# Splitting each unit's wait: products with the high weight part first, those with the low part in the last third

## The reference

```
xn = rmsnorm(h, norm_mix_g)
p_rw, q, c_kv, iq, ik, iw, gates = split(xn @ w_in)         # 2048 -> 9480
h = h + (g_a * (y_a @ w_branch_rwkv) + g_b * (y_b @ w_branch_dsa)) @ w_out
act = gelu(hx . expert_u[e]);  h = h + sum_k gate * act * expert_v[e]   # both expert tables are multiplied whole
q, fz, i, gate = split(rmsnorm(x) @ a_w_in);  x = x + o @ a_w_out
k, v, f = split(rmsnorm(x) @ kv_w);  q, gate = split(rmsnorm(x) @ b_w_in);  x = x + o @ b_w_out
```

## Time and profile before

| what | value |
|---|---|
| median of 3 runs | 3644.63 us |
| profiled execution | 3647.17 us, of which the span from first to last instruction is 3645.0 us |
| granted TensorE clock, mean of the span | 0.983 of full speed |
| PE, matmuls | busy 3546.6 us, 97% of the span, 20474 instructions |
| PE, weight loads | busy 3012.9 us, 83% (they lie beside the matmuls) |
| DVE / ACT / POOL | 59% / 48% / 9% |

### The profile page before, as it was taken

One profiled execution on the slowest core, in us unless ns is written; L12 is line 12 of the kernel. 1 busy time (PEld: TensorE's weight loads), 2 busy tenths in 40 slices (PEclk: granted clock), 3 DMA queues, 4 the chain that ended last, 5 costly groups with the idle time before them and its releaser, 6 DMA issues. The chain is left out here.

```text
span 3645.0 us, 50852 instructions
## 1 busy us (share of the span) xinstructions
PE 3546.6 (97%) x20474; PEld 3012.9 (83%) x20474; DVE 2155.3 (59%) x2871; ACT 1752.3 (48%) x2613; POOL 342.6 (9%) x217
## 2 busy tenths in 40 slices
PE   8998999889999999999999999999999999999999
PEld 6777777678799999888899998887788887788777
DVE  4776555646566487655544465555678885555454
ACT  5453333424444577444444444444555554444763
POOL 0000000000069700000000000000022210000000
PEclk9999999999999999999999999999999999999999
DMA  6554333445545455555555565555544335455334
GB/s 224 176 191 143 116 125 131 160 168 195 189 171 184 173 174 175 193 210 187 193 208 184 207 255 207 207 188 178 175 141 142 133 131 186 177 190 191 127 139 162
DMA packets 111180, 638.55 MB, mean 175 GB/s; under 512 B 17738, under 2 KB 23658, under 8 KB 39192
## 3 DMA queue, kind: packets, MB, share of 16 engines
q1 hardware_dynamic: 106664, 622.98, 48.1%
q0 software_dynamic: 4336, 13.14, 1.1%
HBM read 611.10 MB, written 21.54 MB: 174 GB/s over the span
## 5 line engine op out<-in xcount | busy, mean ns | idle before, releaser
L222 DVE TENSOR_TENSOR lo_w<-ring,hi_w 128x1024 fp32r<-128x1024 f32 x500 | 612.4, 1225 | 989.1 <-ACT hi_w L216 981.2
L216 ACT CAST hi_w<-ring 128x1024 fp32r<-128x1024 f32 x540 | 569.0, 1054 | 958.2 <-DMA ring<-in_wstream 933.6
L224 DVE TENSOR_TENSOR lo_w<-ring,hi_w 128x1024 fp32r<-128x1024 f32 x500 | 612.0, 1224 | 0.0
L1998 PE MATMUL PS<-hi_x,hi_w 128*128 128x256 f32 x2048 | 580.4, 283 | 3.2 <-POOL lo_w L224 3.2
L1998 PE MATMUL PS<-hi_x,lo_w 128*128 128x256 f32 x2048 | 573.9, 280 | 0.0
L1998 PE MATMUL PS<-lo_x,hi_w 128*128 128x256 f32 x2048 | 569.5, 278 | 0.0
L217 ACT CAST hi_w<-ring 128x1024 fp32r<-128x1024 f32 x540 | 564.8, 1046 | 0.0
L2024 PE MATMUL PS<-hi_w,hi_g 128*128 128x512 f32 x1024 | 404.0, 395 | 1.0 <-issue 1.0
L2024 PE MATMUL PS<-lo_w,hi_g 128*128 128x512 f32 x1024 | 403.5, 394 | 0.0
L2024 PE MATMUL PS<-hi_w,lo_g 128*128 128x512 f32 x1024 | 403.2, 394 | 0.0
L1998 PEld LDWEIGHTS PS<-hi_x,hi_w 128*128 128x128 f32 x2048 | 384.8, 188 | 3.6 <-ACT GG L2238 3.5
(11 more groups left out here) (583 smaller groups left out, 5780.0 us busy)
## 6 DMA issues: line engine op xcount, KB each, us to landing
ring<-in_wstream SPq DMA_DIRECT2D x540, 1024.0 KB, 4.8
other_G<-staged SPq DMA_DIRECT2D x32, 256.0 KB, 6.1
hot<-other_G SPq DMA_DIRECT2D x8, 1024.0 KB, 6.9
gates_dram<-gst POOLq DMA_DIRECT2D x8, 512.0 KB, 4.8
x_dram<-x SPq DMA_DIRECT2D x2, 2048.0 KB, 12.0
x<-x_dram SPq DMA_DIRECT2D x2, 2048.0 KB, 9.5
prev<-RKV POOLq DMA_DIRECT2D x6, 508.0 KB, 5.4
x<-in_x SPq DMA_DIRECT2D x4, 512.0 KB, 6.5
```

The costliest lines, as they stand in the source:

```text
L216: a.copy(hi_w[s][:, 0:HALF], ring[s][:, 0:HALF]).then_inc(S(f"hi{s}"), 1)
L222: v.tensor_tensor(lo_w[s][:, 0:HALF], ring[s][:, 0:HALF], hi_w[s][:, 0:HALF].bitcast(F32), ALU.subtract)
L224: v.tensor_tensor(lo_w[s][:, HALF:UNIT], ring[s][:, HALF:UNIT], hi_w[s][:, HALF:UNIT].bitcast(F32), ALU.subtract)\
L1998: m = nc.tensor.matmul(PS[:, s, 0:T], wa[s][:, k * P:(k + 1) * P], xa[:, k, :], start=(k == 0 and p == 0), stop=(k == KC - 1 and p == 2))
```

## The change

Two orders of a dense unit's 24 products are added. `p` is now 0: high x high, 1: low activation x high weight, 2: high activation x low weight.

- `order_lo_last`: tile 0 with p = 0, 1 (8 matmuls), tile 1 with p = 0, 1 (8), then p = 2 of tile 0 (4) and of tile 1 (4).
- `order_by_tile`: as `order_lo_last` within each tile: tile 0's 8 and 4, then tile 1's 8 and 4. It is used for the 8 units of the RWKV branch and for the last unit of the final stage (L3108).

Each unit starts with a wait on `hi{slot}` (both halves), and waits on `lo{slot}` right ahead of its first product with p = 2. In expert-u units the 32 products with `hi_w` come first and then the 16 with `lo_w`; in expert-v units the 16 with `hi_w` and then the 8 with `lo_w`, but for the last unit of a v stage, which waits for both at its start and keeps its bank order. The waits on `psum_free` stand, as before, ahead of the first product of a tile; that of tile 1 is now the 9th product of the unit and was the 13th. The number of matmuls and of weight loads is the same; ACT's, DVE's, POOL's and SP's programs are not touched.

```diff
+    order_by_tile = [(tt, k, p) for tt in range(NT) for ps in ((0, 1), (2,)) for k in range(4) for p in ps]
+    order_lo_last = [(tt, k, p) for ps in ((0, 1), (2,)) for tt in range(NT) for k in range(4) for p in ps]
...
             def quarter(u, g):
...
-                    t.wait_ge(S(f"lo{slot}"), u // SLOTS + 1)
+                    t.wait_ge(S(f"hi{slot}"), u // SLOTS * 2 + 2)
...
-                if WIN + 8 <= u < OUT:
-                    t.wait_ge(S("ya_lo"), 2 * q + tt + 1)
...
-                if g % 2 == 0 and q == 0 and 2 * m + tt >= 3:
-                    before = 2 * m + tt - 3
-                    t.wait_ge(S(f"psum_free{before % 2}"), before // 2 + 1)
-                for k in range(2 * (g % 2), 2 * (g % 2) + 2):
+                by_tile = WIN + 8 <= u < OUT
+                for i, (tt, k, p) in list(enumerate(order_by_tile if by_tile else order_lo_last))[6 * g:6 * g + 6]:
+                    if p == 0 and k == 0:
+                        if by_tile:
+                            t.wait_ge(S("ya_lo"), 2 * q + tt + 1)
+                        if q == 0 and 2 * m + tt >= 3:
+                            before = 2 * m + tt - 3
+                            t.wait_ge(S(f"psum_free{before % 2}"), before // 2 + 1)
+                    if p == 2 and k == 0 and tt == 0:
+                        t.wait_ge(S(f"lo{slot}"), u // SLOTS + 1)
...
             def u_unit(g, s, hf, between=()):
                 t.wait_ge(S("gelu_free"), g * 4 + (hf * HK + s + 1))
-                t.wait_ge(S(f"lo{s}"), g + (GROUP[f"u{hf}"] + 1))
-                for k in range(KC):
+                t.wait_ge(S(f"hi{s}"), g * 2 + (GROUP[f"u{hf}"] * 2 + 2))
+                steps = [(k, p) for k in range(KC) for p in range(2)] + [(k, 2) for k in range(KC)]
+                for i, (k, p) in enumerate(steps):
                     for j in between:
-                        if AT[j] % KC == k:
+                        if 3 * (AT[j] % KC) == i:
                             burst(j)
...
+                    if (k, p) == (0, 2):
+                        t.wait_ge(S(f"lo{s}"), g + (GROUP[f"u{hf}"] + 1))
...
             def v_unit(g, s, hf, first=False, last=False, order=(0, 1)):
-                t.wait_ge(S(f"lo{s}"), g + (GROUP[f"v{hf}"] + 1))
+                if last:
+                    t.wait_ge(S(f"lo{s}"), g + (GROUP[f"v{hf}"] + 1))
+                t.wait_ge(S(f"hi{s}"), g * 2 + (GROUP[f"v{hf}"] * 2 + 2))
...
-                    for p, (ga, wa) in enumerate(((hi_g, hi_w), (hi_g, lo_w), (lo_g, hi_w))):
+                    for p, (ga, wa) in enumerate(((hi_g, hi_w), (lo_g, hi_w), (hi_g, lo_w))[0:3 if last else 2]):
...
+                if not last:
+                    t.wait_ge(S(f"lo{s}"), g + (GROUP[f"v{hf}"] + 1))
+                    for tt, c in pairs:
+                        m = nc.tensor.matmul(PS[:, 4 * tt + c, :], hi_g[:, s, tt * P:(tt + 1) * P],
+                                             lo_w[s][:, c * 512:(c + 1) * 512], start=False, stop=False)
...
             def unit(u):
...
-                t.wait_ge(S(f"lo{q}"), (U0 + u) // SLOTS + 1)
+                t.wait_ge(S(f"hi{q}"), (U0 + u) // SLOTS * 2 + 2)
...
+                for tt, k, p in order_lo_last:
+                    if (k, p) == (0, 0):
+                        if u == KU:
+                            t.wait_ge(S("psum_free1"), N0 + KU // SLOTS - 1)
+                        elif q == 0 and 2 * m + tt >= 3:
+                            before = 2 * m + tt - 3
+                            t.wait_ge(S(f"psum_free{before % 2}"), N0 + before // 2 + 1)
+                    if (tt, k, p) == (0, 0, 2):
+                        t.wait_ge(S(f"lo{q}"), (U0 + u) // SLOTS + 1)
```

More of the change, by code:

```diff
@@ L602, in quarter @@
             def quarter(u, g):
-                slot, tt = u % SLOTS, g // 2
+                slot = u % SLOTS
                 if u < WIN:
@@ L1778, in unit @@
                         t.wait_ge(S(f"psum_free{tt}"), N0 + m - 1)
-                t.wait_ge(S(f"lo{q}"), (O0 + w) // SLOTS + 1)
+                t.wait_ge(S(f"hi{q}"), (O0 + w) // SLOTS * 2 + 2)
                 if w >= QU:
                     t.wait_ge(S("xq_lo"), 2 * q + 2)
[L1782 to L1787, removed]
+                for tt, k, p in order_lo_last:
+                    if (tt, k, p) == (0, 0, 2):
+                        t.wait_ge(S(f"lo{q}"), (O0 + w) // SLOTS + 1)
+                    kk = q * 4 + k
+                    xa, wa = ((X_w[0], hi_w), (X_w[1], hi_w), (X_w[0], lo_w))[p]
+                    mm = nc.tensor.matmul(PS[:, 2 * (m % 2) + tt, :], xa[:, kk, tile(tt)], wa[q][:, k * 512:(k + 1) * 512],
+                                          start=(kk == 0 and p == 0), stop=(kk == KC - 1 and p == 2))
                 mm.then_inc(S("unit_used"), 1)
@@ L2132, in a_unit @@
             def a_unit(u):
-                t.wait_ge(S(f"lo{u}"), A0 // SLOTS + 1)
+                t.wait_ge(S(f"hi{u}"), A0 // SLOTS * 2 + 2)
                 t.wait_ge(S("xa_lo"), 2 * u + 2)
-                for tt in range(NT):
-                    for k in range(4):
-                        kk = u * 4 + k
-                        for p, (xa, wa) in enumerate(((hi_x, hi_w), (hi_x, lo_w), (lo_x, hi_w))):
-                            m = nc.tensor.matmul(PS[:, tt, :], xa[:, kk, tile(tt)], wa[u][:, k * 512:(k + 1) * 512],
-                                                 start=(kk == 0 and p == 0), stop=False)
+                for tt, k, p in order_lo_last:
+                    if (tt, k, p) == (0, 0, 2):
+                        t.wait_ge(S(f"lo{u}"), A0 // SLOTS + 1)
+                    kk = u * 4 + k
+                    xa, wa = ((hi_x, hi_w), (lo_x, hi_w), (hi_x, lo_w))[p]
+                    m = nc.tensor.matmul(PS[:, tt, :], xa[:, kk, tile(tt)], wa[u][:, k * 512:(k + 1) * 512],
+                                         start=(kk == 0 and p == 0), stop=False)
                 m.then_inc(S("unit_used"), 1)
```

82 lines of the change are left out of this document (40 added, 42 removed).

## The result

| | before | changed |
|---|---|---|
| median of 6 runs each | 3642.77 us (3640.19 to 3645.78) | 3658.44 us (3651.55 to 3664.55) |
| ratio, 95% interval | | 1.0039 (1.0027 to 1.0050) |
| profiled execution | 3647.17 us, span 3645.0 | 3663.58 us, span 3661.5 |

The change makes the kernel slower: by 14.2 us as the ratio has it, by 15.7 as the two medians have it. The forecast was +0.7 us and its range ended at 3652. The profiled execution of after is 5 us above its median, so its trace shows a little more loss than the usual run has.

What follows compares the result with a forecast made beforehand. PE, busy 97% of the span, was taken to bound the kernel by products times spacing plus idle time. Terms −0.8 + 0 − 3.2 + 4.65 = +0.7 us on the median 3644.63 gave 3645.3 us, range 3636 to 3652.

Steps and rivals of the forecast that it cites:

- The count and spacing of products: All PE matmuls: same number, and the new order leaves their spacing at 0.2316 us, so 0; ±4 us kept for the range.
- The bound of half a nanosecond: Limit on spacing change per product in dense and v units: 15,960 products x 0.5 ns = ±8 us.
- a count in 350 us off by ten or more: Sign of a wrong forecast: L2024 matmuls begun in 350 us leave 1513 by that much, putting product order on the path.
- The wait for tile 1's bank: Chunk starts in L631 and L2606: bank needed at the 9th product, not the 13th; five late waits of 0.93 us, +4.65.
- the clock behind the longer waits: L2606: longer idle time may drop the clock, 1.7 us per stretch, +5.1 us in all; counted in the range alone.
- L637, taken as 0: Tile 1's bank wait in this line (L631 before): late once, at `RKV`, DVE's chain sets PE's next stop; 0, at most +0.9.
- First unit and expert-u stage: PE starts some 1.4 us earlier in the first unit, −0.8; two 1.6 us waits on POOL's `lo_w` go, −3.2.
- Second `lo_w` wait: At 342.87 us: PE is through earlier but stands longer for DVE before L852; 0, other end −5.1 us.
- One more wait per unit: Some 535 added waits on PE: 0 when already met, at most 2.7 us.
- the second rival: Added wait costs even when met, 0 to 0.08 us per unit: 3656 us at 0.02, 3688 at 0.08; chance 0.12.
- The first rival: Gains kept: idle time at 342.87 us does not return at 358.68, first unit brings more; 3638.5 us or less; chance 0.14.
- the third: Rival: PE waits on `lo_w` just the same, at the 17th product, only the bank wait acts; 3649.3 us; chance 0.08.

Runs made afterwards that it cites:

- order_only: Changed kernel with the wait on the low part back at each unit's start, product order and bank waits kept: 3660.2 us, ratio 1.0052 to the kernel before.
- met_wait: Kernel before, order kept, with one more always-met wait on PE in u, v, L2606 and L3108 units: 3646.51 us, ratio 1.0002.
- v_alternate: Kernel before with 124 steady v units reordered so that neither stationary nor moving block stands twice running: 3641.4 us, ratio 0.9993.
- alternate_all: Kernel before with v_alternate's v units, and dense units of five of six lines changing tile, bank and blocks with every product: 3639.78 us, ratio 0.9983.
- pair_order: Kernel before with v_alternate's sequence of high and low weight parts in dense and v units, tiles and banks as before: 3647.78 us, ratio 1.0014.
- v_runs: Kernel before with 124 steady v units ordered tile by tile in runs of four products keeping one stationary block: 3647.92 us, ratio 1.0007.
- dense_only: Kernel before with only the dense units changed as in the changed kernel, expert units as before: 3655.04 us, ratio 1.0029.
- before_swapped: Kernel before, order and waits untouched, with hi_w and lo_w (with its ring) exchanged in on-chip memory: 3642.77 us, ratio 0.9999.

## Why the prediction was wrong

**The count and spacing of products: 0.** This is the step that failed. It was sized from two orders that both alternate high and low weight parts, product by product; I varied tile and bank in my mind, which turned out to be nothing, and not the run of one part. The bound of half a nanosecond was what those two quotients could hide, not what a new order could do, and it was too narrow even for that: one count more or less in the window of 304 is 0.8 ns, and 216 uninterrupted products of the same stage take 50.15 us, 232.2 ns. In its place: +1.26 ns in 3072 v products (300.39/1297 to 300.39/1290), 3.9 us. For dense units two uninterrupted stretches can be compared, 336 products of the key and value stage (77.95 us, now 78.30) and the 216 behind them (50.15, now 50.31): +0.9 ns, for 6744 products 6.2 us if the others do the same. The second u stage adds 0.4 ns in 3072 products, 1.3 us. Together about 11 us, where the forecast kept 4. By runs, exchanging the places takes back 10.6. The forecast's own sign for this, a count in 350 us off by ten or more, was set too far out: 1506 is off by seven.

**The wait for tile 1's bank: +4.65.** Place and price were right: `fz`, `hq` and `x` grew by 0.9, 0.9 and 2.4 us, 4.2 in all. Removed by experiment it is 7.3 us in that stage and 9.8 with L637 (each uncertain by some 5, so 4.65 is not excluded). What I held for the range alone, the clock behind the longer waits, may be the rest: 3.4 us more of missing clock in after's trace, and about 4 by the means of all runs; neither is beyond what kernels without late banks differ by. L637, taken as 0, had 0.9 at `RKV`, and its share of the 1.8 us at L858.

**First unit and expert-u stage: −0.8 and −3.2.** Right: 19.18 us and no wait on POOL; order_only, which gives them up, is 4.7 us slower.

**Second `lo_w` wait: 0.** Right in kind: a chain of DVE sets PE's next start. But the forecast took DVE's chain as independent of when PE is through, and it isn't: PE's earlier end lets SP load the next unit earlier, that load meets the transfer that DVE waits for, and PE starts 1.8 us later than before. So this term was a loss and not 0.

**One more wait per unit: 0.** Right (met_wait, 1.0002), and with it the second rival fell. The rule of the Trainium skill that weight loads are pulled ahead ("TensorE: Matmul & The Clock Gate", Part 2, step by step) would have let one doubt it; by this case's trace no load was laid bare at a met wait, 1296 products against 1297. The first rival fell with the 12.3 us wait, the third with the 0.8.

The sum with measured terms: −4.7 (splits) + 10.6 (spacing, by place) + 9.8 (banks, with clock) = +15.7, against +14.2 measured. With the uncertainty of each term they would agree over a wide range, so the closeness is partly luck.

## What to carry to other kernels

When an order changes, compare the sequence of operands that PE streams, buffer by buffer, and not only the counts: measure one unit's phases from the starts in the timeline. A spacing term multiplies with every product, so a bound on it must come from an order like the new one, or be as wide as a nanosecond or two. Split a wait only where the profile shows it ending late: the first unit and the first u stage gave the gain, and in the other 530 units the order that the split needs cost time and brought none. And when an engine is to be through earlier, look at what that sets off: here a weight load that met another engine's transfer.

## What the runs showed of the hardware

- In a v unit of after, products of 512 columns that stream from the upper place in on-chip memory start 234.4 ns apart, those from the lower one 230; with the places exchanged it is 235 for the low part (upper place) and 229.4 for the high one. Alternating them hides a part: before has 231.6, the weighted mean of the two phases is 232.9.
- In v units the spacing went with the sequence of the two buffers: with v_alternate's sequence it is 230.0 ns, whatever tiles and banks do (v_alternate, alternate_all, pair_order). It is no full rule: v_runs has one sequence and 232.3 and 233.4 ns in its two halves, and pair_order's dense units have 230.4 ns in one stage and 232.3 in the next.
- The same 48-product u unit of the second u stage, its code, order and places untouched, ran at 117.8 (before, dense_only), 118.5 (v_alternate, v_runs) or 120.0 ns (pair_order) a product over the window of 300 us, and at 119.1 with the places exchanged (before_swapped). What chooses is open; between the ends it is worth 6.7 us a stage, and it took back much of what pair_order and before_swapped had gained.
- A wait that is already met costs PE nothing that nearly 400 of them could show (ratio 1.0002, 0.9993 to 1.0011).
- A 508 KB transfer took 7.1 us from issue to landing where a second 1 MB load was issued ahead of it, and 4.7 us where that load was issued behind it.
